# Final norm spread over three engines, and a later place for a weight split and the squares behind each FFN

## The reference

```
def rms_norm(x, g):
    xf = x.astype(jnp.float32)
    y = xf * lax.rsqrt(jnp.mean(xf * xf, axis=-1, keepdims=True) + EPS)
    return (y * g.astype(jnp.float32)).astype(x.dtype)
```

## Time and profile before

| | us |
|---|---|
| median of 3 runs | 1662.07 (1661.84 to 1668.64) |
| the profiled execution, its own time | 1657.95 |
| its span, first to last instruction | 1656.2 |
| TensorE busy in it | 1571.1 (95%) |
| VectorE, ScalarE, GpSimd busy | 1098.0, 761.3, 460.5 |
| granted TensorE clock, mean | 0.968 |

### The profile page before, as it was taken

How to read it: one execution, slowest core, us unless ns; L and a number is a source line. 1 busy time by engine, 2 the same in 40 slices (tenths; PEclk the granted TensorE clock), 3 DMA queues, 4 the chain that set the end, 5 groups by cost and what they waited for, 6 DMA issues and landing times.

```text
span 1656.2 us, 31321 instructions
## 1 busy us (share of the span) xinstructions
PE 1571.1 (95%) x13050; PEld 1505.9 (91%) x13050; DVE 1098.0 (66%) x1067; ACT 761.3 (46%) x995; POOL 460.5 (28%) x413
## 2 busy tenths in 40 slices
PE   5989998899999999999899999999999998999997
PEld 4989997699999999999889999976999996699996
DVE  7798869957555665566566555645766675476665
ACT  5334360055444544447654343655544455654432
POOL 6999617701000100007540000565100023510000
PEclk8999997699999999999999999999999997999998
DMA  6535540045555465554425555450555542045552
GB/s 214 200 127 203 205 151 26 1 153 176 206 185 195 168 226 184 200 190 166 154 101 182 203 181 201 152 191 1 176 209 186 192 178 77 27 170 211 183 199 76
DMA packets 39027, 265.97 MB, mean 161 GB/s; under 512 B 4352, under 2 KB 6400, under 8 KB 7328
## 3 DMA queue, kind: packets, MB, share of 16 engines
q1 hardware_dynamic: 37808, 261.41, 44.6%
q0 software_dynamic: 1136, 3.38, 0.7%
HBM read 263.70 MB, written 1.06 MB: 160 GB/s over the span
## 4 chain that ended last, share of the span: by engine, by line
PE 83%; DVE 11%; issue 2%; ACT 2%; POOL 2%; DMA 1%; DVEq 0%; SPq 0%; ACTq 0%; POOLq 0%
PE ps L554 77%; DVE gst L1501 3%; PE ps L855 2%; PE ps L845 2%; DVE xlo L1319 2%; DVE wlo L1313 2%; PE ps L833 1%; DVE h L1329 1%; DVE t L1475 1%; DVE t L1476 1%; DMA h<-in_xT 1%; POOL pm L418 1%; PE ps L791 0%; ACT pm L1230 0%; POOL rinv L417 0%
## 5 line engine op out<-in xcount | busy, mean ns | idle before, releaser
L1313 DVE TENSOR_TENSOR wlo<-raw,whi 128x2048 fp32r<-128x2048 f32 x246 | 596.4, 2428 | 220.7 <-ACT whi L995 220.3
L554 PE MATMUL ps<-xhi,whi 128*128 128x256 f32 x2048 | 572.9, 280 | 20.9 <-DVE xlo L1319 13.4
L995 ACT CAST whi<-raw 128x2048 fp32r<-128x2048 f32 x246 | 470.2, 1913 | 243.1 <-PE ps L554 243.0
L554 PE MATMUL ps<-xlo,whi 128*128 128x256 f32 x2048 | 569.6, 278 | 0.0
L554 PE MATMUL ps<-xhi,wlo 128*128 128x256 f32 x2048 | 569.4, 278 | 0.0
L554 PEld LDWEIGHTS ps<-xhi,whi 128*128 128x128 f32 x2048 | 387.8, 189 | 23.9 <-issue 13.4
L554 PEld LDWEIGHTS ps<-xlo,whi 128*128 128x128 f32 x2048 | 388.6, 190 | 0.0
L554 PEld LDWEIGHTS ps<-xhi,wlo 128*128 128x128 f32 x2048 | 387.8, 189 | 0.0
L554 PE MATMUL ps<-hhi,whi 128*128 128x256 f32 x1216 | 335.9, 276 | 0.0
L554 PE MATMUL ps<-hlo,whi 128*128 128x256 f32 x1216 | 335.9, 276 | 0.0
L554 PE MATMUL ps<-hhi,wlo 128*128 128x256 f32 x1216 | 335.9, 276 | 0.0
(11 more groups left out here) (235 smaller groups left out, 2066.8 us busy)
## 6 DMA issues: line engine op xcount, KB each, us to landing
raw<-in_wstream SPq DMA_DIRECT2D x247, 1024.0 KB, 4.8
h<-in_xT SPq DMA_DIRECT2D x1, 1024.0 KB, 8.5
out_hT<-h SPq DMA_DIRECT2D x2, 512.0 KB, 3.0
biasA<-bias_rows POOLq DMA_DIRECT2D x5, 192.0 KB, 5.3
biasB<-bias_rows POOLq DMA_DIRECT2D x3, 192.0 KB, 7.1
braw<-in_s5b POOLq DMA_DIRECT2D x1, 512.0 KB, 4.0
CL<-in_s5c POOLq DMA_DIRECT2D x4, 128.0 KB, 4.3
tg<-in_tgain POOLq DMA_DIRECT2D x1, 384.0 KB, 5.0
```

What stands on the lines that cost most here:

```text
L554: return pe.matmul(o, l, r, start=first, stop=last, skip_group_check=True)
L995: act.copy(whi[:, slot, :], raw[:, slot, :]).then_inc(S("whi_ready"), 1)
L1313: dve.tensor_tensor(wlo[:, slot, :], raw[:, slot, :], whi[:, slot, :], ALU.subtract)\
```

## The change

Five things are altered. (1) At a boundary behind an FFN or behind `mlp0`, ScalarE makes all eight `xhi` tiles first and then the four squares, and `split_lo(F+1)` follows all of VectorE's `x_low`. (2) Behind `s5` and `moba`, and at the kernel's start, the squares of pair 3 follow their `xhi` tiles; behind `ab` and `mla` all stays. (3) In the final norm VectorE sums two of four pairs between the additions to `h`, and TensorE adds up six tiles instead of four. (4) ScalarE multiplies `h` by the gain in place, tile by tile, and VectorE multiplies pairs by `rstd`, four times. (5) Three stores, of 4, 2 and 2 tiles, take the place of two.

```diff
@@ -336,11 +336,11 @@
                     load(NSLOT + n, i, n)
             sp.wait_ge(S("wlo_ready"), N_CHUNKS - NSLOT + 1)
             sp.dma_start(raw[:, N_CHUNKS % NSLOT, :], wstream[0]).then_inc(S(f"raw_landed{N_CHUNKS % NSLOT}"), 16)
-            for g in range(2):
-                t = slice(4 * g, 4 * g + 4)
-                sp.wait_ge(S("out_ready"), 4 * g + 4)
+            for pairs in ((0, 2), (2, 3), (3, 4)):
+                t = slice(2 * pairs[0], 2 * pairs[1])
+                sp.wait_ge(S("out_ready"), pairs[1])
                 sp.dma_start(out.rearrange("(k p) t -> p k t", p=P)[:, t, :], h[:, t, :]).then_inc(S("out_stored"), 16)
-            sp.wait_ge(S("out_stored"), 32)
+            sp.wait_ge(S("out_stored"), 48)
         @block.gpsimd
@@ -974,13 +974,11 @@
             mla_up()
             attention("mla", (6, 7, 0, 1))
             mlp("mlp1")
-            start_stage(10)
-
-            pe.wait_ge(S("final_sums"), 3)
-            for n, j in enumerate((0, 1, 6, 7)):
-                if j == 6:
-                    pe.wait_ge(S("final_sq"), 4)
-                last = mm(ps[:, 7, 0:T], ones[:, :], sq[:, j, :], n == 0, n == 3)
+            pe.wait_ge(S("final_sums"), 2)
+            for n, j in enumerate((0, 1, 4, 5, 6, 7)):
+                if j in (4, 6):
+                    pe.wait_ge(S("final_sq"), j // 2 + 1)
+                last = mm(ps[:, 7, 0:T], ones[:, :], sq[:, j, :], n == 0, n == 5)
             last.then_inc(S("ss_done"), 1)
@@ -997,7 +995,9 @@
             def squares(b):
                 act.activation(sq[:, 2 * b:2 * b + 2, :], h[:, 2 * b:2 * b + 2, :], ACT.Square).then_inc(S("squared"), 1)
-            def x_high(k, before_last=lambda: None):
+            def x_high(k, before_last=lambda: None, squares_after="pair"):
                 if k == 0:
                     act.wait_ge(S("x_loaded"), 16)
@@ -1007,17 +1007,21 @@
                         before_last()
                     if k:
                         act.wait_ge(S("h_ready"), 4 * (k - 1) + b + 1)
-                    if b == 3:
+                    if b == 3 and squares_after == "before":
                         squares(b)
                     for j in (2 * b, 2 * b + 1):
                         act.activation(xhi[:, j, :], h[:, j, :], ACT.Copy, scale=gain(k, j)).then_inc(S("xhi_ready"), 1)
-                    if b < 3:
+                    if squares_after == "pair" or squares_after == "before" and b < 3:
+                        squares(b)
+                if squares_after == "all":
+                    for b in range(4):
                         squares(b)
             def out_projection(st, F):
                 for q in range(3):
                     split_hi(F + q + 2)
-                x_high(NORM_OF[st] + 1, before_last=lambda: split_hi(F + 5))
+                x_high(NORM_OF[st] + 1, before_last=lambda: split_hi(F + 5),
+                       squares_after="before" if st in ("ab", "mla") else "pair")
             def root(k):
@@ -1061,7 +1065,7 @@
                 with act.Fori(1, (FFN_IT - 1) // 2) as i:
                     body(i)
                 split_hi(F + 3 * FFN_IT + 1)
-                x_high(NORM_OF[st] + 1)
+                x_high(NORM_OF[st] + 1, squares_after="all")
             def mlp(st):
                 F = FIRST[st]
@@ -1289,11 +1293,22 @@
             mla_up()
             attention("mla")
             mlp("mlp1")
+            def with_gain(j):
+                act.activation(h[:, j, :], h[:, j, :], ACT.Copy, scale=gain(10, j)).then_inc(S("final_gain"), 1)
             for b in range(4):
                 act.wait_ge(S("h_ready"), 36 + b + 1)
                 act.activation(sq[:, 2 * b:2 * b + 2, :], h[:, 2 * b:2 * b + 2, :], ACT.Square)\
                     .then_inc(S("final_sq"), 1)
+                if b in (1, 2):
+                    act.wait_ge(S("final_sq"), b)
+                    with_gain(2 * b - 2)
+                    with_gain(2 * b - 1)
+            act.wait_ge(S("final_sq"), 4)
+            for j in (4, 5, 6):
+                with_gain(j)
             root(10)
+            with_gain(7)
         @block.vector
@@ -1319,21 +1334,36 @@
                 dve.scalar_tensor_tensor(out=xlo[:, j, :], in0=h[:, j, :], scalar=gain(k, j), in1=xhi[:, j, :],
                                          op0=ALU.mult, op1=ALU.subtract).then_inc(S("xlo_ready"), 1)
-            def advance(k, scale, banks, landed, before):
+            def advance(k, scale, banks, landed, before=lambda b: None):
                 for b in range(4):
-                    if k < N_NORMS - 1:
-                        before(b)
+                    before(b)
                     dve.wait_ge(*landed(b))
                     hb = h[:, 2 * b:2 * b + 2, :]
                     dve.scalar_tensor_tensor(out=hb, in0=bank2(banks[b]), scalar=scale, in1=hb, op0=ALU.mult,
                                              op1=ALU.add).then_inc(S("h_ready"), 1)
-                    if k < N_NORMS - 1 and b:
+                    if b:
                         x_low(k, 2 * b - 2)
                         x_low(k, 2 * b - 1)
-                if k < N_NORMS - 1:
-                    x_low(k, 6)
-                    x_low(k, 7)
+                x_low(k, 6)
+                x_low(k, 7)
+            def advance_last(k, landed):
+                for b in range(4):
+                    dve.wait_ge(*landed(b))
+                    hb = h[:, 2 * b:2 * b + 2, :]
+                    dve.tensor_tensor(hb, bank2(b), hb, ALU.add).then_inc(S("h_ready"), 1)
+                    if b == 1:
+                        dve.wait_ge(S("final_sq"), 1)
+                        dve.tensor_tensor(sq[:, 0, :], sq[:, 0, :], power[:, 2:3].to_broadcast([P, T]), ALU.add)\
+                            .then_inc(S("final_sums"), 1)
+                    if b == 2:
+                        dve.wait_ge(S("final_sq"), 2)
+                        dve.wait_ge(S("final_sums"), 1)
+                        dve.tensor_tensor(sq[:, 0:2, :], sq[:, 0:2, :], sq[:, 2:4, :], ALU.add)\
+                            .then_inc(S("final_sums"), 1)
             def inverse_root(k):
@@ -1396,7 +1426,8 @@
                 with dve.Fori(1, (FFN_IT - 1) // 2) as i:
                     body(i)
                 n = F + 3 * FFN_IT
-                advance(k + 1, 0.5, range(4), acc_landed(st, n), lambda b: split_lo(n + 1) if b == 1 else None)
+                advance(k + 1, 0.5, range(4), acc_landed(st, n))
+                split_lo(n + 1)
             def mlp(st):
                 F, k = FIRST[st], NORM_OF[st]
@@ -1410,7 +1441,11 @@
                         hidden(st, 1 + u, i, (1 + u) % 3, 3, c)
                         split_lo(c + 3, i)
                 n = F + 2 * MLP_IT
-                advance(k + 1, 1.0, range(4), acc_landed(st, n), lambda b: split_lo(n + 1) if b == 1 else None)
+                if k + 1 < N_NORMS - 1:
+                    advance(k + 1, 1.0, range(4), acc_landed(st, n))
+                    split_lo(n + 1)
+                else:
+                    advance_last(k + 1, acc_landed(st, n))
             def out_projection(st, F, banks):
                 advance(NORM_OF[st] + 1, 1.0, banks, lambda b: (S("w_used"), F + b + 1),
@@ -1639,18 +1674,11 @@
             mla_up()
             attention("mla", (6, 7, 0, 1))
             mlp("mlp1")
-            dve.wait_ge(S("final_sq"), 1)
-            dve.tensor_tensor(sq[:, 0, :], sq[:, 0, :], power[:, 2:3].to_broadcast([P, T]), ALU.add)\
-                .then_inc(S("final_sums"), 1)
-            for b in (1, 2):
-                dve.wait_ge(S("final_sq"), b + 1)
-                dve.wait_ge(S("final_sums"), b)
-                dve.tensor_tensor(sq[:, 0:2, :], sq[:, 0:2, :], sq[:, 2 * b:2 * b + 2, :], ALU.add)\
-                    .then_inc(S("final_sums"), 1)
             inverse_root(10)
-            for j in range(KT):
-                dve.scalar_tensor_tensor(out=h[:, j, :], in0=h[:, j, :], scalar=gain(10, j), in1=rstd[:, :],
-                                         op0=ALU.mult, op1=ALU.mult).then_inc(S("out_ready"), 1)
+            for b in range(4):
+                hb = h[:, 2 * b:2 * b + 2, :]
+                dve.wait_ge(S("final_gain"), 2 * b + 2)
+                dve.tensor_tensor(hb, hb, both(rstd[:, :]), ALU.mult).then_inc(S("out_ready"), 1)
```

## The result

The changed kernel takes 1682.34 us in the median (1679.33 to 1687.97, 4 runs), the kernel before 1661.95 beside it (4 runs): ratio 1.014, 95% interval 1.0115 to 1.0164. It is slower by 20.4 us; the forecast was 19.5, at 1681.5.

What follows compares the result with a forecast made beforehand. TensorE, 83% of the span, was taken as the bound, its waits at stage boundaries and the end as where the change works. Boundaries +15.8, clock +8 and end -4.3 gave +19.5, put on the median: 1681.5 us, range 1667 to 1688.

Steps and rivals of the forecast that it cites:

- VectorE and GpSimd exclude each other: At boundaries: either engine's begun operation keeps the other out to its end; statistics 15.8 us later in sum over the stages.
- The gain on VectorE: Behind FFNs and mlp0: without the early split TensorE goes through chunk F unbroken, 2.2 us earlier.
- The clock: TensorE's clock falls after idle gaps in s5, moba, ab and mla: 2.0 us per gap, +8 for four.
- The end: Final norm: TensorE goes straight on, -3.4 us; four products for eight, -0.75; smaller last store, -0.15; together -4.3.
- only one split in the chain: Rival, at the boundaries: only one split gets into GpSimd's chain of adds; +7, 1669 us; chance 0.13.
- the adds do not stand still: Rival, at the boundaries: GpSimd's adds do not stand still behind splits; -7.4, 1654.7 us; chance 0.08.

Runs made afterwards that it cites:

- experiment 7: Changed kernel with both splits (F+1 and F+2) held on VectorE until GpSimd's last add is done: 1676.75 us, ratio to before 1.0107.
- experiment 4: Changed kernel with only split F+2 held on VectorE until GpSimd's last add is done: 1675.61 us, ratio to before 1.0112.
- experiment 5: The filler: changed kernel with 205 unused matmuls ahead of TensorE's wait for the sum in s5, moba, ab, mla: 1670.2 us, ratio to before 1.0073.
- experiment 2: Changed kernel with split F+1 early again, ahead of pair 1, behind FFNs and MLPs; squares stay late: 1682.18 us, ratio to before 1.0143.
- experiment 3: Changed kernel with the squares back between the xhi tiles behind FFNs and mlp0; split F+1 stays late: 1655.48 us, ratio to before 0.9973.
- experiment 8: Kernel before with the new end and, behind ffn1 alone, squares behind all xhi with split F+1 early: 1657.04 us, ratio 0.9978.
- experiment 6: Kernel before with the new end; behind ffn1 squares late, split F+1 early; behind ffn2 and ffn3 only split F+1 late: 1654.92 us, ratio 0.9973.

## Why the prediction was right

**VectorE and GpSimd exclude each other: right.** The forecast rested on one pair of rows and said where each split would fall in the chain. The last add was put 16.2 us after the first addition and came at 15.95; experiments 7, 4 and the changed kernel, with none, one and two splits among the adds, give 12.0, 13.9 and 15.95. The Trainium skill (SBUF — State Buffer, shared port pair) says that the loser fully blocks; the trace agrees: 0.61 for an epsilon add alone, 2.71 beside a split.

**The gain on VectorE: right.** Chunk F is done 2.2 us earlier in every stage, and only ffn2, where statistics stand behind chunk F+1, keeps some: -1.1, forecast -0.85. Statistics in moba came 4.2 us later (forecast 4.6), in s5 2.5 (2.85).

**The clock: right in kind, too small.** I put 2.0 us on each of four gaps, 8 in all. The filler gave back 11 to 13. In s5 and moba 4.0 us ran at half clock, 2.0 lost as taken. In ab it was 6.3, about 3 lost, beyond the end that I had given (2.4), and in mla most of the stretch that follows. The error of the step is that the price of a gap was taken from the two gaps shown, while it depends on when the clock comes back, and in a stage that itself stops and starts, like mla, it may not come back before the next stop. The Trainium skill's example (TensorE: Matmul & The Clock Gate, HAM oscillation), 1.67 us throttled a stall and half of it lost, would give 3.3 for four; here the measurement is over three times that, and decides.

**What the forecast didn't hold.** s5 lost 2 us more than forecast. TensorE gets the result of the last scan 125.5 us after ffn0's first addition, 4.2 later than in the kernel before (121.3); from there to the stage's end it works without a gap, and takes 2.6 us longer. The windows of this work shown above give most of that: 3.0 us at a granted clock of 0.50 and the next 29.0 at 0.99 are 1.8 us lost by my estimate. This is a clock loss that the prediction did not have: the clock fell in the stage's scans, over 100 us behind the boundary. The filler doesn't touch it: in experiment 5, 3.0 us run at 0.50 at the same place, and so they do in experiment 4. Why the clock is back in time in one version and not in the other stays open. The 1.0 us of ffn1 is no effect of the change: with the changed kernel's order ahead of it ffn1 took 191.95 us in five experiments (2 to 5 and 7), and with before's order 193.2 in experiment 8. The start up to ffn0's end takes from 211.8 to 216.1 us in the profiles of the changed kernel and of experiments 2 to 5 and 7, whose start is the same, with no step of mine to answer for it.

**The end: right.** -3.7 in the span where -4.3 was forecast. TensorE runs on into the statistics at full clock, the reciprocal comes 3.2 earlier (3.4), four products for eight give 0.75 (0.75). The smaller last store gave nothing (0.15 forecast): 256 KB land in 3.2 us where 512 KB take 3.0, and of the 4.0 us by which the last product is earlier the span's end keeps 3.7.

That the sum came out within a microsecond owes much to luck. The profiled span moved by 24.1 where the terms had 19.5: the table's differences to the forecast are 1.9 in s5, 3.1 in mla, 1.0 in ffn1, 0.5 in ab and 0.6 at the end too little, against 1.7 in ffn0, 0.5 in moba and 0.3 in ffn2. The medians moved by 20.4. Of the rivals, "only one split in the chain" is what experiment 4 builds, and "the adds do not stand still" what experiment 7 builds by hand; the changed kernel is neither.

## What to carry to other kernels

A recorded duration longer than the same instruction's elsewhere is a wait that no table of waits shows: if it is on VectorE or GpSimd, look at what the other of the two does beside it, and count about one full instruction of that as the price (2.0 us here for a split of 2.29). When work is moved later so that it disturbs nobody, write down what runs at its new place, and whether VectorE and GpSimd are both in it. An idle TensorE costs its gap and then the clock; where the gap can't go, matmuls in it may be worth trying (11 to 13 us here).

## What the hardware showed that I had not expected

- TensorE's clock can fall while it is busy: in experiment 3, 0.93 over 2.3 us and 0.50 over the next 3.0, both busy throughout, after 0.9 us of idle; in the kernel before the same stretch of mla stayed at 1.00.
- A version that alters nothing in a stage but the moment of its start can change that stage by 2 to 4 us: ab took 118.1 us in the kernel before and 120.2 in experiment 8, with one order at its boundary, and 117.9 and 121.9 in experiments 3 and 6, with another.
- Filler matmuls of no use made the kernel 12 us faster (1682.34 to 1670.2).
- The clock can be lost far behind the place that was changed: at the end of s5, 3.0 us at 0.50, in the changed kernel and with the filler alike.
